# Moving the remainder of one weight unit on VectorE from in front of the residual addition to behind the norm, in a two-block transformer kernel

## What is computed

```python
for l in range(DEPTH):                                   # DEPTH = 2
    x = x + 0.5 * swiglu(rms_norm(x, ffn1_norm[l]), ffn1_w1[l], ffn1_w3[l], ffn1_w2[l])
    h = rms_norm(x, mix_norm[l])
    z = h @ w_in[l]                                      # 1024 x 6752: all projections of the mixer
    ...                                                  # three attention branches, gates, w_out
    x = x + 0.5 * swiglu(rms_norm(x, ffn2_norm[l]), ffn2_w1[l], ffn2_w3[l], ffn2_w2[l])
```

## Time and profile before

| | us |
|---|---|
| median of 3 runs | 1929.99 |
| lowest and highest of the 3 | 1925.03 and 1934.77 |
| the profiled execution, its own time | 1937.23 |
| its span, from the first to the last instruction | 1935.4 |

### The profile page before, as it was taken

One profiled execution on the slowest core, in us unless ns is written; L12 is line 12 of the kernel. 1 busy time (PEld: TensorE's weight loads), 2 busy tenths in 40 slices (PEclk: granted clock), 3 DMA queues, 4 the chain that ended last, 5 costly groups with the idle time before them and its releaser, 6 DMA issues. The chain is left out here.

```text
span 1935.4 us, 27285 instructions
## 1 busy us (share of the span) xinstructions
PE 1753.4 (91%) x11146; PEld 1555.9 (80%) x11146; DVE 1031.2 (53%) x1186; ACT 808.1 (42%) x1054; POOL 236.0 (12%) x222
## 2 busy tenths in 40 slices
PE   7999999999899979999998998999977878778786
PEld 7999787878799979998886888899977666577664
DVE  4544566654654535445565646554546554465553
ACT  5343555533434334344464523434334324334342
POOL 0000410100000000000410100000005900049000
PEclk9999999999999999999999998999988878888788
DMA  7557453423455536566452414455535311254210
GB/s 230 198 183 223 142 193 104 131 66 131 135 192 189 180 109 195 179 204 211 151 168 88 131 66 132 151 196 181 187 101 173 132 54 44 72 168 140 79 44 33
DMA packets 207751, 275.07 MB, mean 142 GB/s; under 512 B 19015, under 2 KB 168233, under 8 KB 207145
## 3 DMA queue, kind: packets, MB, share of 16 engines
q1 hardware_dynamic: 205800, 272.66, 43.1%
q10 hardware_dynamic: 1856, 1.06, 0.2%
HBM read 271.61 MB, written 1.08 MB: 141 GB/s over the span
## 5 line engine op out<-in xcount | busy, mean ns | idle before, releaser
L301 DVE TENSOR_TENSOR wlo<-raw,whi 128x2048 fp32r<-128x2048 f32 (+1 forms) x258 | 580.3, 2252 | 556.5 <-ACT whi L290 556.1
L290 ACT ACTIVATE whi<-raw 128x2048 fp32r<-128x2048 f32 (+1 forms) x258 | 483.9, 1878 | 332.7 <-PE bank L366 118.8
L366 PE MATMUL bank<-hT_hi,whi 128*128 128x256 f32 x1408 | 401.6, 285 | 5.6 <-DVE hT_lo L241 5.6
L366 PE MATMUL bank<-hT_lo,whi 128*128 128x256 f32 x1408 | 400.9, 285 | 0.0
L366 PE MATMUL bank<-hT_hi,wlo 128*128 128x256 f32 x1408 | 400.8, 285 | 0.0
L366 PEld LDWEIGHTS bank<-hT_hi,whi 128*128 128x128 f32 x1408 | 272.9, 194 | 8.4 <-DVE wlo L301 6.3
L366 PEld LDWEIGHTS bank<-hT_lo,whi 128*128 128x128 f32 x1408 | 272.9, 194 | 1.4
L366 PEld LDWEIGHTS bank<-hT_hi,wlo 128*128 128x128 f32 x1408 | 272.8, 194 | 0.0
L379 PE MATMUL bank<-whi,Y 128*128 128x512 f32 x704 | 223.9, 390 | 0.0
L379 PEld LDWEIGHTS bank<-whi,Y 128*128 128x128 f32 x704 | 132.3, 188 | 26.7
L379 PE MATMUL bank<-wlo,Y 128*128 128x512 f32 x352 | 137.4, 390 | 0.0
(11 more groups left out here) (383 smaller groups left out, 2950.9 us busy)
## 6 DMA issues: line engine op xcount, KB each, us to landing
raw<-in_ffn_w SPq DMA_DIRECT2D x132, 1024.0 KB, 5.3
raw<-in_w_in SPq DMA_DIRECT2D x80, 1024.0 KB, 5.4
raw<-in_w_out SPq DMA_DIRECT2D x16, 1024.0 KB, 4.9
raw<-in_w_br_na SPq DMA_DIRECT2D x4, 1024.0 KB, 5.7
raw<-in_w_br_mla SPq DMA_DIRECT2D x4, 1024.0 KB, 5.1
raw<-in_w_br_gla SPq DMA_DIRECT2D x4, 1024.0 KB, 5.0
raw<-in_cmp_k_w SPq DMA_DIRECT2D x4, 1024.0 KB, 7.5
raw<-in_cmp_v_w SPq DMA_DIRECT2D x4, 1024.0 KB, 5.3
```

The source lines that it names most:

```text
L290: act.activation(m["whi"][:, slot, 0:w], m["raw"][:, slot, 0:w], ACT.Copy).then_inc(s.hi_ready, 1)
L301: dve.tensor_tensor(m["wlo"][:, slot, 0:w], m["raw"][:, slot, 0:w], m["whi"][:, slot, 0:w].bitcast(F32), ALU.subtract).then_inc(s.lo_ready, 1)
L366: mm = pe.matmul(B[bank][:, mt * T:(mt + 1) * T], a, b, start=(n == 0 and k == 0), stop=(n == KK - 1 and k == 2))
```

## The change

The remainder of unit 34 is no longer made at the end of `FFN.dve`, in front of the residual, but after the eight remainders of `hT`. Every semaphore keeps its order of counts.

```diff
@@ class FFN, dve @@
                 r.dve_low(dve, base + 4, sl(4))
                 hid_low(h, j)
         triple(FF_PAIRS - 2)
-        r.dve_low(dve, u0 + FFN_UNITS + 1)
 
     def dve_add(self, dve, t, x_ready):
@@ first_layer, block.vector @@
                     norm.dve_scale(dve, 1, t)
                 for kk in K_ORDER:
                     norm.dve_low(dve, 1, kk, gain[1])
+                ring.dve_low(dve, UM + 1)
 
                 def proj(i):
```

## The result

| | before | after |
|---|---|---|
| median of 20 runs each, us | 1929.07 | 1936.43 |
| lowest and highest | 1925.03 and 1934.77 | 1927.67 and 1940.83 |
| ratio after/before, 95% interval | | 1.0035, 1.0025 to 1.0046 |
| profiled execution: own time, span | 1937.23, 1935.4 | 1939.59, 1937.8 |
| mean granted clock of TensorE | 0.938 | 0.932 |

The changed kernel is slower by 0.35%, some 6.7 us. I had forecast -0.1 us. The difference is clear of zero and lies beyond the upper bound of the sum, +3.6 us. The measured time is inside the stated range only because the scatter of the runs had been added to that bound; that is luck and no merit of the forecast.

The account below looks back on a forecast made before the run. TensorE, busy 91% of the span, was taken as the bound. Two places of -0.05 us for the norm and 0 for remainder, queue and clock gave -0.1 us (bounds -2.4 and +3.6), so 1929.9 us, range 1922.5 to 1938.

Parts of the forecast that it names:

- Tile 1's additions: In the residual, they wait for TensorE's end already, so the norm gains 0.05 us a place, at most 0.09.
- Unit 34's remainder was in time: Behind hT's remainders it ends before TensorE's first weight load of unit 34, slack 0.6 and 0.9 us: 0 us, at most 0.1.
- GpSimd's longer run: Mask additions lose another 2.1 us and end near 228, hidden by GpSimd's idle time until 235.81: no cost.
- the late load: Unit 37's load is issued 12.5 us later, near 216.2, and lands 2.8 us before ScalarE takes it up: no cost.
- The remainders beside GpSimd: Behind the norm, each takes 2.35 to 2.63 us, against 2.29 alone; one meeting a mask addition loses at most 0.69 us.
- The clock: TensorE's half-clock stretch around the norm's transposes: taken as 0 us, between 1.1 us won and 1.7 us lost a place.
- the slow clock lasts longer: Rival: at both places TensorE, with two gaps instead of one, stays slow longer: 2 x 1.7, or 1933.4 us; chance 0.07.
- the first gap becomes shorter: TensorE's gap ahead of the transposes: argument given against a longer slow clock; no size of its own.
- the rival of a late unit 34: Rival: TensorE waits for unit 34's remainder at its first weight load, 1.5 and 1.2 us late: +2.7 us; chance 0.14.

Follow-up runs that it names:

- experiment 2: Kernel before with unit 34's remainder made twice, uncounted in front of the residual and counted behind the norm: 1930.18 against 1929.85 us, ratio 1.0002.
- experiment 3: Kernel before with unit 34's high part and remainder kept in front of the residual but made in two halves: 1932.68 against 1929.85 us, ratio 1.0020.
- experiment 6: Changed kernel with 4 unread matmuls between the transposes of tile 0 and tile 1: 1926.06 us against 1930.84 for the kernel before, ratio 0.9982.
- experiment 7: Kernel before again with no edit, one execution for a second trace: 1935.38 us.
- experiment 18: Changed kernel with 4 unread matmuls between the mixer norm's transpose groups and 12 ahead of the second feed-forward norm's: 1927.49 against 1930.05 us for before, ratio 0.9983.
- experiment 11: Changed kernel with no edit, one execution for a fourth trace: 1934.83 us.
- experiment 8: Kernel before with no edit, one execution for a third trace: 1932.16 us.

## Why the prediction was wrong

**Right.** Tile 1's additions were bound by TensorE's end, so that taking the remainder away brought the norm 0.16 us (3.67 - 3.51) and not 1.5; I had put 0.05 and no more than 0.09. Unit 34's remainder was in time, GpSimd's longer run and the late load were hidden, and experiment 2 shows no cost of them together. The remainders beside GpSimd behaved as priced: the first two of the three took 5.04 us together, against 2 x 2.29 = 4.58 undisturbed, so they lost 0.5 us, less than one mask addition. (The longest remainder in the traces of both kernels took 2.87 us, more than the 2.63 that I had gone by; that of unit 34 was done at least 0.5 us in time at all ten places of the changed kernel.)

**The step that failed** is "The clock": "Between them I take 0, nearest to the row as it stands." The row is the earlier trace rows, TensorE's granted clock of 0.50 for 3.25 us, behind its one idle stretch of 3.02 us; that half of a slow stretch's length is won or lost was an estimate from that 0.50. The runs show in its place a half clock that lasts 6.8 us and not 3.4 at 7 of the 10 places of the changed kernel (1 of 10 before), which made the places 0.73 and 0.76 us longer in the mean, and more time at half clock in the first layer's mixer, 2.31 us of length, for which the sum had no term. I had the right mechanism as a rival (the slow clock lasts longer, 2 x 1.7, +3.4 us) with a chance of 0.07, and argued against it that the first gap becomes shorter. The table of starts shows that the length of one gap isn't what counts. Where a second gap split TensorE's work, the stretch was 6.8 us long for every start between 2.5 and 3.8 us, where the single gap left it at 3.4. It was long in 8 of 12 places with the split, and in 2 of 16 without. With a long one the place takes 13.6 to 14.2 us as I measure it, with a short one 12.2 to 12.9. So the price of the rival, 1.7 us for each place with the long stretch, was nearly right (1.4 us between the middles of these two), and its chance of 0.07 was not. Two figures beside it were slips: from 209.1 to 211.5 it is 2.4 us and not 2.2, and the rival of a late unit 34 adds up to 2.6 us and not 2.7. Neither matters for what failed.

Averages over five traces of each kernel, in us:

| | before | after | difference |
|---|---|---|---|
| first place | 12.85 | 13.58 | +0.73 |
| mixer of the first layer | 287.59 | 289.90 | +2.31 |
| second place | 12.80 | 13.56 | +0.76 |
| mixer of the second layer | 290.12 | 290.31 | +0.19 |
| own time of the profiled executions | 1932.64 | 1936.67 | +4.03 |

**The term that the sum lacked** is in the second row of this table: nothing was changed inside the mixer, and it took 2.3 us more in the first layer. There, too, it is the clock: 20.5 to 23.9 us at half clock in all five traces of the changed kernel, 6.8 to 17.1 in the five of before. At about 316 us, in the attention, the stretches by time are, of the kernel before and then of the changed one:

```profile
317.40:324.00 6.60, 6.60 (x22) 4.78 (x21) 2.90 (x8) 3.44 (x11) 0.00 (x0) 0.50 0.35 143
```

```profile
316.30:326.30 10.00, 9.35 (x32) 7.04 (x33) 4.53 (x12) 4.52 (x11) 0.00 (x0) 0.50 0.31 107
```

What makes one trace of a program differ from the next isn't shown. The stretches start 2.32 to 4.20 us behind TensorE's end in the five traces of the kernel before and 2.40 to 4.18 us in those of the changed one, and the mixers took 285.3 to 291.3 and 289.0 to 291.3 us. No run here sets the start.

**What the mixer's loss goes with.** Call **lead** the time from the end of the slow stretch at a place to the start of unit 34's first matmul. These are all 26 places in the traces of both kernels and of experiments 2, 3 and 6, with what the mixer behind each had:

| lead, us | stretch at the place, us | at half clock in the mixer, us | length of the mixer, us | places |
|---|---|---|---|---|
| 3.2 to 3.4 | 6.8 | 20.5, and 23.9 in 4 | 289.7 to 291.0 | 4 changed, 1 of experiment 3 |
| 3.7 to 3.9 | 6.8 | 20.5 in all | 289.0 in all | 3 changed |
| 4.2 | 6.8 | 6.8 | 285.3 | 1 before |
| 4.9 to 5.0 | 3.4 | 23.9 in all | 291.1 to 291.3 | 3 before, 2 changed, 1 each of experiments 2 and 3 |
| 5.1 to 5.3 | 3.4 | 17.1 in all | 288.1 to 289.0 | 4 before, 1 each of experiments 2 and 6 |
| 6.0 to 6.4 | 3.4 | 13.7, and 20.5 in 1 | 287.1 to 290.2 | 2 before, 1 changed, 1 of experiment 6 |

At leads of 4.9 to 5.0 us, which both kernels have, the mixer is equally long in either, so the change shows no cost of its own inside the mixer. What it alters is the lead: a long stretch left 3.2 to 3.9 us in the changed kernel, and all mixers behind such leads had 20.5 us or more at half clock. It also fits that the second layer lost so little, 0.19 us: there the kernel before itself had leads of 4.9 to 5.0 us, with 23.9 us at half clock behind them, in three of its five traces.

**What stays open.** The table is read from traces and no run set the lead, so that it shows what the mixer's time goes with, not that it must follow. Why the mixer had 6.8 us at half clock behind a lead of 4.2 us and 23.9 behind one of 4.9 us isn't known. The timed runs give the change 6.7 and 5.6 us by their ratios, the five traces 4.0; with single executions 10 us apart, the rest may be scatter.

## What to carry to other kernels

Where TensorE idles for a few microseconds in a serial step such as a norm, look at the granted clock of the rows behind it before moving anything into or out of the gap. Starting half of the next work earlier, without the other half, may split the gap and hold the clock down for longer (here a gap of 3.02 us became two of 2.04 and 0.50 to 1.12, and 7 places of 10 had 6.8 us at half clock, against 1 of 10 before), and the loss then falls on matmuls that wait for nothing. Where a gap can't be closed, it is worth trying matmuls that nobody reads; four of them in the second gap took back the whole loss here. And where single executions lie 10 us apart, one trace of each kernel is not enough to say what a change of a few microseconds does.

## What the runs showed of the hardware

- In an unchanged stretch of the program, the mixer of the first layer, the same kernel had from 6.8 to 17.1 us at half clock from one execution to the next, and its length went from 285.3 to 289.0 us. The row of 217 to 505 us, of the first trace and of experiment 7 (the granted clock is the third figure from the end):

```profile
217.00:505.00 288.00, 269.25 (x1694) 233.67 (x1693) 171.98 (x239) 132.17 (x190) 29.17 (x20) 0.97 0.39 126
217.00:505.00 288.00, 268.12 (x1709) 232.89 (x1708) 172.04 (x239) 133.87 (x191) 28.30 (x20) 0.99 0.41 130
```

- A stretch of half clock can begin while TensorE is already at work again: in experiment 2, 3.75 us behind the end of the feed-forward part and 0.7 us behind the first transpose.
- A gap of 2.04 us on TensorE was followed by half clock at all ten places of the changed kernel, as one of 3.02 us was at all ten of the kernel before. With the second gap filled (experiments 6 and 18) it was at three places of four.
- A mask addition on GpSimd and a remainder on VectorE take longer side by side: the addition 0.68 to 0.73 us without a remainder beside it and up to 2.83 with one (once 5.00, in experiment 11), the remainder 2.29 us without GpSimd and up to 2.87 beside the additions (experiment 8).
